# Key norm's root moved off GpSimd, upper heads' keys turned first, cross attention's query roots as a scale per token

## What is computed

```python
def rms_norm(x, g):
    xf = x.astype(jnp.float32)
    y = xf * lax.rsqrt(jnp.mean(xf * xf, axis=-1, keepdims=True) + EPS)
    return (y * g.astype(jnp.float32)).astype(x.dtype)
...
    kv = (ckv @ lp['w_mla_kvb']).reshape(B, S, MLA_HEADS, MLA_NOPE + MLA_V)
    kn = rms_norm(kv[..., :MLA_NOPE], lp['g_k_nope'])
...
def cross_attend(h, mk, mv, lp):
    q = rms_norm((h @ lp['w_xq']).reshape(B, T, X_HEADS, X_DIM), lp['g_xq'])
    s = jnp.einsum('bthd,bnhd->bhtn', q, mk).astype(jnp.float32) * (X_DIM ** -0.5)
    p = jax.nn.softmax(s, axis=-1).astype(mv.dtype)
```

## Time and profile before

| | us |
|---|---|
| median of three runs (lowest, highest) | 1236.36 (1234.31, 1237.33) |
| the profiled execution's own time | 1235.52 |
| its span, first to last instruction | 1233.7 |
| PE busy | 1184.5 (96%) |
| PE weight loads busy | 1056.4 (86%) |
| DVE busy | 620.8 (50%) |
| ACT busy | 381.0 (31%) |
| POOL busy | 298.4 (24%) |

### The profile page before, as it was taken

How to read it: one execution, slowest core, us unless ns; L and a number is a source line. 1 busy time by engine, 2 the same in 40 slices (tenths; PEclk the granted TensorE clock), 3 DMA queues, 4 the chain that set the end, 5 groups by cost and what they waited for, 6 DMA issues and landing times.

```text
span 1233.7 us, 22574 instructions
## 1 busy us (share of the span) xinstructions
PE 1184.5 (96%) x8132; PEld 1056.4 (86%) x8132; DVE 620.8 (50%) x1036; ACT 381.0 (31%) x875; POOL 298.4 (24%) x181
## 2 busy tenths in 40 slices
PE   7999999899999999999989977999999999999997
PEld 4799896576989999999867754699999999999997
DVE  0659553876566656666431255444454444444443
ACT  4222024355544444454301246233320002331000
POOL 0126043710566565565702100110000000000000
PEclk9999999989999999999999989999999999999999
DMA  8432102120242222222025222132222222222202
GB/s 336 151 103 91 35 2 61 35 71 9 57 167 76 73 59 52 51 74 73 1 74 199 69 69 69 35 105 84 85 82 81 77 85 86 86 84 73 65 0 77
DMA packets 62629, 97.44 MB, mean 79 GB/s; under 512 B 22961, under 2 KB 41554, under 8 KB 62482
## 3 DMA queue, kind: packets, MB, share of 16 engines
q1 hardware_dynamic: 61970, 94.56, 24.0%
q0 software_dynamic: 576, 1.84, 0.4%
HBM read 91.12 MB, written 5.25 MB: 78 GB/s over the span
## 4 chain that ended last, share of the span: by engine, by line
PE 79%; DVE 5%; issue 4%; POOL 3%; ACT 3%; SPq 3%; DMA 1%; POOLq 0%; DVEq 0%; ACTq 0%
PE bank L1343 33%; PE bank L713 8%; PE bank L775 6%; PE bank L793 4%; PE bank L1144 3%; POOL stat L2615 3%; PE bank L1146 3%; PE bank L1145 3%; PE bank L737 2%; PE bank L1096 2%; PE bank L1172 2%; PE bank L1034 2%; SPq L627 1%; PE bank L1076 1%; PE bank L1054 1%
## 5 line engine op out<-in xcount | busy, mean ns | idle before, releaser
L1343 PE MATMUL bank<-hr,wr 128*128 128x288 f32 x1536 | 205.2, 296 | 1.0 <-DVEq L2292 1.0
L1343 PEld LDWEIGHTS bank<-hr,wr 128*128 128x128 f32 x1536 | 204.9, 189 | 1.4 <-issue 1.4
L1343 PE MATMUL bank<-ur,wr 128*128 128x288 f32 x1536 | 205.3, 296 | 0.0
L1343 PEld LDWEIGHTS bank<-ur,wr 128*128 128x128 f32 x1536 | 205.0, 189 | 0.1
L2615 POOL TENSOR_TENSOR stat<-stat,cst 128x32 f32<-128x32 f32 x32 | 173.7, 5428 | 2.5
L1144 PE MATMUL bank<-wq_high,c_parts 128*128 128x288 f32 x512 | 162.3, 317 | 3.5 <-ACT hT L1651 2.5
L1146 PE MATMUL bank<-wq_low,c_parts 128*128 128x288 f32 x512 | 151.5, 296 | 0.0
L1145 PE MATMUL bank<-wq_high,c_parts 128*128 128x288 f32 x512 | 150.6, 294 | 0.0
L2401 DVE CAST wr<-ring 128x1024 fp32r<-128x1024 f32 x64 | 44.4, 694 | 209.3 <-PE bank L1343 208.6
L2184 DVE TENSOR_REDUCE stat<-hT 128x8 f32<-128x512 f32 x128 | 86.9, 684 | 78.2 <-ACT hT L1651 74.2
L1144 PEld LDWEIGHTS bank<-wq_high,c_parts 128*128 128x128 f32 x512 | 96.5, 188 | 8.2 <-ACT hT L1651 3.9
(11 more groups left out here) (392 smaller groups left out, 1878.1 us busy)
## 6 DMA issues: line engine op xcount, KB each, us to landing
ring<-in_ring_w_dram SPq DMA_DIRECT2D x106, 512.0 KB, 3.5
arena<-in_cache_ckv_dram SPq DMA_DIRECT2D x128, 128.0 KB, 2.0
arena<-in_cache_mk_dram SPq DMA_DIRECT2D x8, 512.0 KB, 3.4
arena<-in_cache_mv_dram SPq DMA_DIRECT2D x8, 512.0 KB, 9.2
mixT<-in_x_dram SPq DMA_DIRECT2D x1, 2048.0 KB, 12.6
arena<-in_cache_kpe_dram SPq DMA_DIRECT2D x128, 16.0 KB, 1.6
out_dram<-hT SPq DMA_DIRECT2D x4, 512.0 KB, 3.2
mixT<-in_w_qb_dram SPq DMA_DIRECT2D x1, 1152.0 KB, 5.8
```

Source lines behind the costliest of these rows:

```text
L1343: ins = mm(outs[c][:, 0:HALF], w[:, ew, k, :], src[:, ex, k0 + k, c * HALF:(c + 1) * HALF], start=(start and k == 0 and n == 0), stop=(sto ...
```

## The change

1. **Key norm.** DVE adds epsilon to the 40 sums (L2072 of the new kernel), ACT takes logarithm and exponential of them behind its copies of the first query tile, DVE refines with three small operations. The multiplication of `kfull` moves from ahead of the first `query_sums` to ahead of the third. POOL no longer has a part in it.
2. **Turning.** Keys of heads 4 to 7 come first. ACT's wait for the written states moves behind the six first banks. `absorbed(1)` and `qpd` come before the last values and queries. Ahead of attention PE waits for keys and values only, and for a head's queries at its first step (t = 0).
3. **Cross attention.** A head is no longer scaled by its root. DVE copies each half out of PSUM with the gain, ACT squares the same half straight out of PSUM behind it. The sums of squares are formed with tokens on partitions: the squares are the stationary operand, 8 columns of ones the moving one, for heads 0 and 1 between projections 2 and 3, for heads 2 and 3 (and the samples) in the second step of the pair loop. ACT and DVE take the roots of 128x8 and 128x10 numbers. A root then enters as the scale operand of the exponential, and DVE multiplies the row maximum by it (a small operation more for every pair of maxima, prompt and sample).

```diff
 TURNED_ORDER = (
-    *(("kT", h) for h in range(4)), ("vp", 0), "qTs", *(("kT", h) for h in range(4, MH)), ("vp", 1), ("qabs", 0),
-    ("qT", 0), ("qT", 1), ("vp", 2), ("qT", 2), ("qT", 3), ("qT", 4), ("qT", 5), ("vp", 3), ("qT", 6), ("qT", 7),
-    ("qabs", 1), "qpd")
+    *(("kT", h) for h in range(4, MH)), ("vp", 0), "qTs", *(("kT", h) for h in range(4)), ("vp", 1), ("qabs", 0),
+    ("qT", 0), ("qT", 1), ("vp", 2), ("qabs", 1), ("qT", 2), ("qT", 3), ("qT", 4), ("qT", 5), "qpd", ("vp", 3),
+    ("qT", 6), ("qT", 7))
...
-            for key in [("kT", h) for h in range(MH)] + [("vp", t) for t in range(4)] + [("qT", h) for h in range(MH)]:
+            for key in [("kT", h) for h in range(MH)] + [("vp", t) for t in range(4)]:
...
+                    if t == 0:
+                        b, i = PLAN[("qT", h)]
+                        pe.wait_ge(bank_free[b], i)
...
+            def query_squares(u):
+
+                pe.wait_ge(S("acc"), KD - 1 + 2 * u + 2)
+                o = reopen(pe, ("ms_xq", u))
+                for t in range(4):
+                    for e in range(2):
+                        n = 2 * t + e
+                        ins = mm(o[:, 8 * n:8 * n + 8], mixT[:, 2 * u + e, t * P:(t + 1) * P], ones[:, 0:8],
+                                 start=True, stop=True)
...
+                    if n == 0:
+                        act.wait_ge(S("ss_mla"), TILES + 1)
+                        link(A(stat[:, 232:272], stat[:, 192:232], ACT.Ln))
+                        A(stat[:, 232:272], stat[:, 232:272], ACT.Exp, scale=-0.5).then_inc(S("root"), 1)
...
-            act.wait_ge(S("state_in"), 32)
             act.wait_ge(S("gon"), 5)
-            for h in range(4):
+            for h in range(4, MH):
                 turned_keys(h)
...
+            act.wait_ge(S("state_in"), 32)
+            for h in range(4):
                 turned_keys(h)
...
+            for j in range(XH):
+                for c in range(2):
+                    o = full(act, ("xq", j, c))
+                    act.wait_ge(S("xq"), 2 * j + c + 1)
+                    A(mixT[:, j, c * HALF:(c + 1) * HALF], o[:, 0:HALF], ACT.Square).then_inc(S("sq_xq"), 1)
...
-                          bias=stat[:, 2 * n + e:2 * n + e + 1],
+                          bias=stat[:, 2 * n + e:2 * n + e + 1], scale=r_xq[u][:, 2 * t + e:2 * t + e + 1],
...
+                    top = stat[:, 2 * n:2 * n + 2]
+                    link(V.tensor_reduce(top, o[:, :].rearrange("p (e c) -> p e c", e=2), AX.X, ALU.max, negate=True))
+                    if n in (0, 3):
+                        query_roots(n // 3)
+                    V.tensor_tensor(top, top, r_xq[u][:, 2 * t:2 * t + 2], ALU.mult).then_inc(S("cmax"), 1)
...
-            link(G.tensor_tensor(stat[:, 232:272], stat[:, 192:232], epsk.broadcast_to([P, 40]), ALU.add))
-            G.tensor_tensor(stat[:, 232:272], stat[:, 232:272], power.broadcast_to([P, 40]), ALU.pow).then_inc(
-                S("r_mla"), 1)
```

More of the change, by code:

```diff
@@ L205, in make_plan @@
                 turn(("wo", j, c))
-    for j in range(XH + 1):
+    for j in range(XH):
         for c in range(2):
[L209 to L213, removed]
+            turn(("xq", j, c))
+        if j == 2:
+            turn(("ms_xq", 0))
+    fill(("ms_xq", 1), 0)
     for n in range(8):
@@ L1010, in _ @@
             value_rows(2)
+            absorbed(1)
             for h in range(2, 6):
                 turned_queries(h)
[L1013 to L1016, removed]
             pe.wait_ge(S("qp4"), 1)
@@ L1021, in _ @@
             filled(ins, "qpd")
+            value_rows(3)
+            for h in range(6, MH):
+                turned_queries(h)
             arrive(pe)
-            for key in [("kT", h) for h in range(MH)] + [("vp", t) for t in range(4)] + [("qT", h) for h in range(MH)]:
+            for key in [("kT", h) for h in range(MH)] + [("vp", t) for t in range(4)]:
                 b, n = PLAN[key]
@@ L1592, in _ @@
             act.nop().then_inc(S("qTs"), 1)
-            for h in range(4, MH):
+            act.wait_ge(S("state_in"), 32)
+            for h in range(4):
                 turned_keys(h)
@@ L2092, in _ @@
                 if n == 1:
-                    dve.wait_ge(S("r_mla"), 3)
+                    dve.wait_ge(S("root"), roots["k"] + 1)
+                    m, r = stat[:, 192:232], stat[:, 232:272]
+                    link(V.scalar_tensor_tensor(out=m, in0=m, scalar=-0.5, in1=r, op0=ALU.mult, op1=ALU.mult))
+                    link(V.tensor_tensor(m, m, r, ALU.mult))
+                    link(V.scalar_tensor_tensor(out=r, in0=m, scalar=1.5, in1=r, op0=ALU.add, op1=ALU.mult))
+                    dve.wait_ge(S("r_mla"), 2)
+                if n == 3:
                     k8 = kfull.rearrange("p t (h c) -> p (t h) c", h=MH)
@@ L2125, in _ @@
             absorbed(0)
-            for h in range(1, MH, 2):
-                turned_queries(h)
+            turned_queries(1)
             absorbed(1)
+            turned_queries(3)
+            turned_queries(5)
             dve.wait_ge(S("pads"), 5)
@@ L2312, in _, with query_roots @@
             add_to_x("wo", "x_mix", [(j, 0) for j in range(4)] + [(j, 1) for j in range(4)] + in_turn[8:], gained)
-            def query_head(j):
+            for j in range(XH):
                 for c in range(2):
-                    refine(("ms_xq", j, c), mixT[:, 4 + j, c * HALF:(c + 1) * HALF], roots["xq"] + 2 * j + c + 1)
-                V.scalar_tensor_tensor(out=xqT[:, j, :], in0=xqT[:, j, :], scalar=gxq,
-                                       in1=mixT[:, 4 + j, :], op0=ALU.mult, op1=ALU.mult).then_inc(S("xq"), 1)
-            for j in range(XH - 1):
-                query_head(j)
+                    o = full(dve, ("xq", j, c))
+                    n = 2 * j + c + 1
+                    V.tensor_scalar(xqT[:, j, c * HALF:(c + 1) * HALF], o[:, 0:HALF], gxq, None, ALU.mult).then_inc(
+                        S("xq"), 1)
+                    dve.wait_ge(S("xq"), n)
+            def query_roots(u):
+                dve.wait_ge(S("root"), roots["xq"] + u + 1)
+                m, r = m_xq[u], r_xq[u]
+                link(V.scalar_tensor_tensor(out=m, in0=m, scalar=-0.5, in1=r, op0=ALU.mult, op1=ALU.mult))
+                link(V.tensor_tensor(m, m, r, ALU.mult))
+                link(V.scalar_tensor_tensor(out=r, in0=m, scalar=1.5, in1=r, op0=ALU.add, op1=ALU.mult))
             pairs = [(t, u) for u in range(2) for t in range(4)]
```

110 lines of the change are left out of this document (54 added, 56 removed).

## The result

| | before | after |
|---|---|---|
| median (7 runs each) | 1236.36 us | 1229.3 us |
| lowest, highest | 1234.31, 1239.3 | 1226.9, 1231.25 |
| ratio, 95% interval | | 0.9939 (0.9927 to 0.9952) |
| profiled execution's own time, span | 1235.52, 1233.7 | 1230.8, 1229.0 |

A forecast was written before the change was run, and what follows sets the result against it. PE was taken to bound nearly everything, so only its pauses counted. Gains of 1.5 + 6.2 = 7.7 us took the profiled 1235.5 to 1227.8; the median, 0.8 above, gave 1228.7 us, range 1226.5 to 1231.5, chance 0.52.

The forecast's parts named there:

- term 1: Keys, turning and attention's first steps: a gain of 1.5 us, bounds 0 to 3.
- term 2: Cross attention: a gain of 6.2 us, bounds 3 to 8.
- The low stretch behind the pause: Ahead of attention, behind PE's pause for POOL's root: the lower clock level costs 1.5 us in the following 9.6 us.
- The order of these 9.6 us changes, not their sum: From the queries' transposes to attention: PE's work is reordered but takes the same total time.
- Behind these waits only attention is queued on PE: At attention's start: its first step needs head 6's queries, copied 0.7 us after PE's end, which is no later.
- (a): No low clock spells in either place: 1225.7 us, up to 2.5 lower if attention's pause costs no clock; chance 0.15.
- The scale operands: Cross attention's exponentials: 0.1 us more each, two per step on the chain, 1.6 us in all.
- Behind both places PE has no wait that would take the gain back: After the keys' part and cross attention: the gains stay, since page loads start from the same semaphores.
- (b): Cross attention's narrow products don't overlap: 7.5 us more, 1236.2 us, no change; chance 0.10.
- (c): Ahead of attention, POOL stretches DVE's multiplication of the keys by sharing SBUF: 1231.0 us; chance 0.12.
- (d): Cross attention's loop falls to the low clock level, costing 14 us: 1242.7 us, slower; chance 0.05.
- (e): Only the keys' gain arrives, cross attention being held by something unseen: 1234.9 us; chance 0.06.

The follow-up runs named there:

- e1: The kernel before with points 1 and 2 of the change (key norm, turning), cross attention as before: 1235.14 us, ratio 0.9987.
- c1: The new kernel unchanged, measured and profiled again on a second occasion: 1227.9 us, ratio 0.9928.
- e4: The new kernel with 22 added identity transposes filling PE's 3.1 us pause ahead of the query transposes: 1226.8 us, ratio 0.9929.
- e2: The kernel before with only point 3 of the change (cross attention): 1230.85 us, ratio 0.9963.
- e8: The kernel before with the keys' root on ACT and DVE and the later multiplication, old turning order and waits: 1231.64 us, ratio 0.9975.
- e5: The new kernel without the scale operand in cross attention's exponentials, leaving the queries' roots out of the result: 1224.41 us, ratio 0.9904.
- e10: The new kernel with 16 added identity transposes in the 2.13 us pause ahead of cross attention's first sample values: 1225.98 us, ratio 0.9931.
- e3: The new kernel with the keys' multiplication two tiles earlier, directly behind the refined root: 1226.65 us, ratio 0.9925.

## Why the prediction was right, step by step

The forecast was 1228.7, the median 1229.3, and 7.7 us of gain stand against 7.5. The mechanism held in both places. But term 1 came out 1.3 us larger and term 2 1.5 us smaller, so that the sum is this close is luck.

**Term 1** was to be 1.5 us, and is 2.8 by the stages of e1 (1.9 in the trace after).
- The mechanism held. DVE's wait vanished at no cost, and PE's pause moved behind the keys: 3.4 us forecast, 3.13 measured, released by POOL. The queries' transposes were forecast for 241.5 and start at 241.54.
- The low stretch behind the pause was forecast at -1.5; A grew by 1.61. The wait ahead of attention was to fall by 0.5 and fell from 1.36 to 1.05 us (0.89 in c1). A shows nothing of it, because "The order of these 9.6 us changes, not their sum" doesn't hold. Without any low time the row from the first query transposes to the last takes 244.05 to 253.62 before, 9.57 us, and 10.93 - 0.89 = 10.04 in e4. Why the same products take 0.5 us more in the new order isn't shown. Attention starts at 254.08, not 253.5.
- The step that failed is that the sum ends at "Behind these waits only attention is queued on PE" and puts the clock of attention's first steps at nothing. Rival (a) names it ("up to 2.5 lower"), the sum doesn't. Before, the pause of 1.36 us ahead of attention was followed by 6.8 us at the low level (e2 shows the same; e8 3.4 us of it). In no trace with the new order does that come, and P is 53.26 instead of 54.92: +1.66 us. It stood in plain sight in the trace of before. That it would go away didn't: no run here shows what takes it away.

**Term 2** was to be 6.2 us, and is 4.7.
- Up to keys 3 it held closely. Projection 3 was to end at 719.0 (keys 0 start at 719.12), and keys 1 to start at 722.1 (722.12). Narrow products were put at 2.2 us for 32 records and take 728.46 - 726.43 = 2.03. Keys 3 were forecast 9.3 earlier, less 1.5 for a low stretch in the filling, and start 7.86 earlier in the trace that has this stretch.
- The scale operands were to cost 1.6 and cost 1.1 up to the end of the pair loop (761.09 - 754.33 = 6.76 us are left of the 7.86). The pace of 3.75 is there, and e5 shows its cause.
- The step that failed is "Behind both places PE has no wait that would take the gain back": the loop's gain was to reach the output projection whole. The pause ahead of the samples' values grew by 0.37 us, since the samples' last exponentials are slower as well, and at 2.13 us it is followed by the low level: -1.6 (e10). I had one low stretch for cross attention, two came, and the second is the new kernel's own. Of 9.3 - 1.6 - 1.5 = 6.2 us are left 7.86 - 1.10 - 0.37 - 1.6 = 4.8. The bound of 3 us for two of them was in my range of this term.

**Rivals.** (a) *No low spells* doesn't come as such; each pause has its own odds. Its time, 1225.7, is about what the new kernel reaches in its fastest executions (1226.9, 1225.47). (b) falls: full narrow products follow each other at 0.11 us. (c) falls: the multiplication of the keys takes 2.29 us next to a busy POOL. But the one 0.82 us among the 0.42 of L2078, which the prediction passed over, was a sign of what (c) is about (see the last section). (d) falls: the granted clock is 1.00 from 735 to 740. (e) falls: e2 by itself gains 4.6 us. Their chances were added up with a slip: b and e are 0.16, not 0.15.

**What I should have done.** I costed pauses in idle time and then guessed a clock price for the stage. The trace of before allows better: each pause of PE above 1 us, with what follows it, is a row, and those rows give the price of a pause that an edit makes, lengthens or removes.

## What to carry to other kernels

In a kernel that PE bounds nearly throughout, count its pauses, not the other engines' waits: a pause costs its length and often 1.6 us more behind it at the lower clock level. An operation that only has to be early enough belongs into the gap of its engine: the keys' multiplication, moved to where DVE waits anyway, shortened Q by 1.3 us. When a releaser is taken away, follow each engine to the one that is late next, and carry the sum on to the end of the next stage, since the first change of the clock behind a landmark may hold as much as the landmark itself. Run each part of a change by itself, too: the new order of turning came with the root, and no run here shows that it pays.

## What the hardware showed beyond what I had expected

- *Two engines at SBUF.* While DVE's multiplication with two inputs runs from 224.58 for 2.29 us, POOL's scaling beside it takes 2.49 us instead of 0.61 (224.85 above). In e3, where the multiplication runs beside an idle POOL, the same scaling takes 0.62. The last one (240.37) takes 1.12 beside DVE's scaling of 0.69 us, which began at 240.32. In these two pairs DVE began first and its time doesn't move. In a third pair POOL began first, and DVE's operation takes 0.82 us instead of 0.42:

```profile
236.30 0.61 POOL L2612 TENSOR_TENSOR hT<-hT,stat 128x256 f32<-128x256 f32 x1
236.38 0.82 DVE L2101 TENSOR_TENSOR ring<-hT 128x256 f32<-128x256 f32 x1
```

The kernel before has the same pair at 237.85 and 237.93. In all three the engine that began second pays. The Trainium skill (GPSIMD Engine Reference, 1. Specifications) says that the two share their interfaces and contend when DVE has two SBUF inputs; the traces agree. I had put the price of the multiplication on DVE, and there it falls on POOL.
- *Products with 8 moving columns.* 16 with weights of 128x128 follow each other at (728.20 - 726.43) / 16 = 0.11 us, as the earlier trace rows let expect. 16 with weights of 128x32, in four groups of rows, at (728.46 - 728.20) / 16 = 0.016 us, though a record of either says 0.17 to 0.26.
- *The same pause, not the same clock.* The pause of 2.29 us at the end of the pages, with another of 0.78 behind it, is in all fourteen traces; the low level is found behind it in eight and not in six. A single trace of either kernel can be off by 1.6 us a stretch: the two profiled executions differ by 4.7 us, the medians by 7.1.
